# One load for all sample histories in a hybrid convolutional decoder step on eight cores

## The chip, the cores and the metric

The kernel runs on all 8 cores of one Trainium2 chip, one program per core on its own part of the data; the cores do not exchange anything. The time of a run is the device time of the slowest core, in microseconds. Three runs of the kernel before gave a median of 884.12 us (883.93 to 884.82). Each core has TensorE (PE, matmuls), VectorE (DVE), ScalarE (ACT), GpSimd (POOL), SyncE (SP) and 16 DMA engines, which all queues share. DMAs are issued here from SP (the hardware queue, no change of type) and from POOL (the software queue, which can turn f32 into bf16 on the way).

## The reference, cut to what matters

Width is 1024, the depthwise kernel has 31 taps. The change touches only branch B's input for the sample sequences: 128 sequences of 8 new tokens, each with 30 carried rows of history.

```python
a_b, a_c, a_h, a_z, b_v, b_g, b_z, gate_a, gate_b = split(rmsnorm(h) @ w_in)
s  = a_c * a_h;  ya = a_b * dwconv3([buf_a, s]) * silu(a_z);          ya = ya @ w_out_a
v  = b_v * sigmoid(b_g)
ext_b = concatenate([buf_b, v], axis=1)      # history rows in front: zeros for prompts, state_conv_b for samples
c  = dwconv31(ext_b) + b_conv_b
yb = (silu(layernorm(c)) * silu(b_z)) @ w_out_b
h  = h + (sigmoid(gate_a) * ya + sigmoid(gate_b) * yb) @ w_o
h  = h + sigmoid(rmsnorm(h) @ w_pg) * (p @ w_pe);   y = rmsnorm(h)
```

## The kernel before, in words

Each core has 2176 tokens: one prompt of 2048 tokens, in four chunks (`si` 0 to 3) of 512 tokens each, and 16 sample sequences with 128 tokens (`si` 4). Channels are in 8 blocks `j` of 128. The order of all work is the order in which the Python code calls `S.add`; each engine runs its own instructions in that order and waits on semaphores for the others, so an instruction that waits holds everything behind it on its engine.

- **Start (0 to about 73 us).** x tiles are loaded into `xs1`, scaled to bf16 in `xb1`, transposed by PE and stored as `uT`. Both buffers lie in the upper half of `cb`, which is not yet in use. Between the tiles PE does the first projections.
- **v projections.** `s2_proj(j, si)` multiplies chunk `si` by the two weight tiles of block `j` (slots of the ring of 8, loaded by POOL), DVE forms v (L535) in `vrow`, and SP stores it to DRAM (`vd<-t_vrow`). Blocks 0 to 3 are done first (the loop over `PIECES`), blocks 4 to 7 are interleaved with the convolution. When the last chunk of block `j` is projected, `wdone` frees its two ring slots and `pump` issues the next two weight loads on POOL.
- **The convolution** works on `v8[j % 2]`, which has a row for each 16 channels times 8 phases, in 8 groups q, of 340 columns: 4 zeros, 256 of the prompt (`t_v<-vd`, SP, L566), and columns 260 to 339 for the samples, 16 sequences times 5. Of the five, the first four are history and the last is the new token. `hist_load(j)` (L557, POOL) loads all 80 columns from DRAM; then a DVE copy, `conv_samples(j)` (L578, L580), overwrites every fifth with the new token from `vs8`. `conv_half(j, hh)` (L596, L604) does 20 matmuls per half, 16 halves in all; ACT copies the result (L611) and SP moves it into `cb` (`t_cb<-t_c`). `v8` has two buffers, so block `j` can be loaded only when the convolution of block `j - 2` has been read by PE.
- The list `POS` (L1058) sets after which of the 20 projection jobs each half stands. `conv_samples(0)` stands ahead of the third job's projection, `s2_proj(4, 1)`; the first half stands right behind that projection.
- `swq` (L337) lets at most 6 DMAs of the software queue be under way: each waits until the sixth before it has landed.
- **Afterwards** come branch A with its taps, the LayerNorm statistics, the output projections and the last stage by token tiles (about 731 us to the end). None of that code is changed.

`alias(new, old)` makes the first writer of a name wait for all that used the old names of the same memory.

Of the kernel before, what the change touches and what calls it, by code (L numbers as in the profile page):

```python
# [8 lines left out]
BF16 = mybir.dt.bfloat16  # L9
# [4 lines left out]
NCH = 8  # L14
# [3 lines left out]
NTOK = 2176  # L18
# [5 lines left out]
NPH = 8  # L24
NBL = 256
NQ = 8
# [130 lines left out]
def build_program():  # L157
    nc = bass.Bass("TRN2", target_bir_lowering=False)

    def din(name, shape):  # L160
        return nc.dram_tensor(name, shape, F32, kind="ExternalInput").ap()
# [4 lines left out]
    x_d = din("x", [NTOK, D])  # L166
    pT_d = din("pT", [128, 2, NTOK])
    sa_d = din("sa", [128, NCH, 32])
    h8_d = din("h8", [NCH, 128, NQ, 80])
    sbh_d = din("sbh", [352, D])  # L170
    w_in = din("w_in", [72, 128, D])
    w_oa = din("w_oa", [8, 128, D])
# [21 lines left out]
    with contextlib.ExitStack() as st:  # L194
# [5 lines left out]
        def at(name, shape, dt, off):  # L200
            n = size_of[dt]
            for s in shape[1:]:
                n *= s
            assert off % 32 == 0 and off + n <= SIZE - 64, (name, off, n)
            return nc.alloc_sbuf_tensor_at("t_" + name, shape, dt, offset=BASE + off)
# [3 lines left out]
        def take(n):  # L209
            o = cur[0]  # L210
            cur[0] += (n + 31) // 32 * 32
            return o

        def sb(name, shape, dt):
            n = size_of[dt]
            for s in shape[1:]:
                n *= s
            return at(name, shape, dt, take(n))
# [3 lines left out]
        o_cb = take(NCH * NTOK * 4)  # L222
# [35 lines left out]
        v8 = [sb(f"v8{i}", [128, NQ, 340], BF16) for i in range(2)]  # L258
# [25 lines left out]
        o_r4 = o_cb + 4 * NTOK * 4  # L284
        NXS = 6
        xs1 = [at(f"x1{i}", [128, D], F32, o_r4 + 4096 * i) for i in range(NXS)]
        NXB = 4
        xb1 = [at(f"xb1{i}", [128, D], BF16, o_r4 + 4096 * NXS + 2048 * i) for i in range(NXB)]
        X1_RES = [f"x1{i}" for i in range(NXS)] + [f"xb1{h}{i}" for i in range(NXB) for h in ("", "h")]


# [15 lines left out]
        S = Sched(nc)  # L307
# [3 lines left out]
        def balloc():  # L311
            return free_banks.pop(0)
# [24 lines left out]
        def swq():  # L337
            r = f"swq{swq_ctr[0] % SWQ}"
            swq_ctr[0] += 1
            return r  # L340

        def pdma(out, in_, reads, writes, key):
            S.add("pool", lambda e: e.dma_start(out=out, in_=in_), reads=reads, writes=list(writes) + [swq()], dma=key)  # L343

        def sdma(out, in_, reads, writes, key):
            S.add("sp", lambda e: e.dma_start(out=out, in_=in_), reads=reads, writes=writes, dma=key)  # L346
# [49 lines left out]
        def wgroup():  # L396
            g = gnext[0]
            gnext[0] += 1
            assert all(t in slot_of for t in WG[g]), "weight tile not prefetched"
            return g, [slot_of[t] for t in WG[g]]  # L400

        def wdone(g):
            for t in WG[g]:
                ring_free.append(slot_of[t])
            pump()
# [7 lines left out]
        def proj(b, k_ring, si, o=0, n=None):  # L413
            n = n or CHUNKS[si][1]
            tt = range(4 * si + o // 128, 4 * si + (o + n) // 128)
            res = [f"uT{t}" for t in tt], [f"uT{t}" for t in tt] + [f"uTh{t}" for t in tt]
            mm8(b, k_ring, lambda k: uT[si][:, k, o:o + n], lambda k: res[k // 4], n)
# [136 lines left out]
            bfree(bg, bv)  # L554


        def hist_load(j):  # L557
            s = j % 2
            pdma(v8[s][:, :, 260:340], h8_d[j], [], [f"v8{s}h"], f"v8{s}h")

        def conv_load(j):
            s = j % 2
            if j >= 2:
                hist_load(j)
            if j < 7:
                sdma(v8[s][:, :, 4:260], vd[j].rearrange("c (a m) -> (c a) m", m=NBL).rearrange("(q r) m -> r q m", r=128),  # L566
                     [f"vd{j}_{si}" for si in range(4)], [f"v8{s}p"], f"v8{s}p")
            else:
                for q in range(NQ):
                    sdma(v8[s][:, q, 4:260], vrow[16 * q:16 * q + 16, :].rearrange("c (a m) -> c a m", m=NBL),  # L570
                         [f"vst{i}" for i in range(NVST)], [f"v8{s}p"] if q == 0 else [f"v8{s}p{q}"], f"v8{s}p{q}")
# [5 lines left out]

        def conv_samples(j):  # L578
            s = j % 2
            S.add("dve", lambda e: e.tensor_copy(out=v8[s][:, :, 264:340:5], in_=vs8[s][:]),  # L580
                  reads=[f"vs8{s}"], writes=[f"v8{s}h"])
            if j + 2 < NCH:
                vs_pend.append(j + 2)
# [140 lines left out]
        def s3_job(j, si):  # L724
            off, n = CHUNKS[si]
            if j not in s3w:
                s3w[j] = wgroup()
            g, (kh, kc, kz, kb) = s3w[j]
            bh, bc, bz, bb = [balloc() for _ in range(4)]
            for b, kk in ((bh, kh), (bc, kc), (bz, kz), (bb, kb)):  # L730
                proj(b, kk, si)
            if si == 4:
                wdone(g)
            th = talloc()
            S.add("act", lambda e: e.activation(out=tmp[th][:, 0:n], in_=ps[:, bh, 0:n], func=AF.Copy),  # L735
                  reads=[f"ps{bh}"], writes=[f"tmp{th}"])
            if si < 4:
                sdst, sres = sxf[:, 512 + off:512 + off + n], f"sx{si}"
            else:
                S.add("pool", lambda e: e.tensor_copy(out=sexts[:, 0:32], in_=hista[:, j, :]),  # L740
                      reads=["hista"], writes=["sextsh"])
                sdst, sres = sexts[:, 32:160], "sextsn"
            S.add("dve", lambda e: e.tensor_tensor(out=sdst, in0=ps[:, bc, 0:n], in1=tmp[th][:, 0:n], op=ALU.mult),  # L743
                  reads=[f"ps{bc}", f"tmp{th}"], writes=[sres])
            if si == 3:
                S.add("pool", lambda e: e.tensor_copy(out=sx[:, 0:2, 1:NBL], in_=sx[:, 8:10, 0:NBL - 1]),
                      reads=["sx3"], writes=["sxh"])
                S.add("pool", lambda e: e.tensor_copy(out=skeep[:, j, :].unsqueeze(2), in_=sx[:, 8:10, NBL - 1:NBL]),
                      reads=["sx3"], writes=[f"skeep{j}"])
            if si == 4:  # L750
                S.add("pool", lambda e: e.tensor_copy(out=skeep_s[:, j, :], in_=sexts[:, 128:160]),
                      reads=["sextsn"], writes=[f"skeep_s{j}"])
            tz = talloc()
            S.add("act", lambda e: e.activation(out=tmp[tz][:, 0:n], in_=ps[:, bz, 0:n], func=AF.Silu),
                  reads=[f"ps{bz}"], writes=[f"tmp{tz}"])
            if si == 3:
                zap, zres = bzh[:, 0:n], "bzh"
            else:
                zap, zres = tmp[tz][:, 0:n], f"tmp{tz}"
            S.add("dve", lambda e: e.tensor_tensor(out=zap, in0=ps[:, bb, 0:n], in1=tmp[tz][:, 0:n], op=ALU.mult),  # L760
                  reads=[f"ps{bb}", f"tmp{tz}"], writes=[zres])
            bfree(bh, bc, bz, bb)
            if si != 3:
                taps(j, si, zap, zres)
            if si == 2:
                taps(j, 3, bzh[:], "bzh")
# [262 lines left out]
        for p, (si, o, n, prep) in enumerate(PIECES):  # L1029
            for j in range(4):  # L1030
                if si == 3 and 1 <= j < 3:
                    conv_load(j - 1)
                s2_proj(j, si, o, n)
                if si == 3 and o + n == 512:
                    wdone(s2w[j][0])
                if prep[j]:
                    s1_step()
                if si == 3 and o == 0 and builds:
                    w_build(*builds.pop(0))
                if si == 2 and o == 0 and j < 2:  # L1040
                    hist_load(j)
                    vs_load(j)
            if p == 0:
                S.add("pool", lambda e: e.memset(onesf, 1.0), writes=["onesf"])
                S.add("pool", lambda e: e.memset(epsc[:], LN_EPS), writes=["epsc"])
                for i in range(2):
                    S.add("pool", lambda e, i=i: e.memset(v8[i][:, :, 0:4], 0.0), writes=[f"v8{i}z"])
                for j in range(4):
                    vsd_store(j)
                pdma(mask[:], mask_d, [], ["mask"], "mask")  # L1050
                pdma(tw.rearrange("p a b -> p (a b)"), tw_d, [], ["tw"], "tw")
                sdma(hista[:], sa_d, [], ["hista"], "hista")
        S.alias([f"cq{q}_{g}" for q in range(4, 8) for g in range(NQ)] + [f"c{q}_4" for q in range(4, 8)], X1_RES)

        jobs = [(j, si) for j in range(4, 8) for si in (4, 0, 1, 2, 3)]
# [51 lines left out]


        conv_samples(7)
        s3_job(0, 3)  # L1110
        for _ in range(2):
            half()
# [50 lines left out]
        j = NCH - 1  # L1163
# [131 lines left out]
```

How the kernel before makes its waits and increments, by code:

```python
            def run(engname, e):  # L113
                waited = {}
                for o in ops:
                    if o["eng"] != engname:
                        continue
                    need = {}
                    for d in o["deps"]:
                        od = ops[d]
                        v = od["seq"] * (16 if od["dma"] is not None else 1)
                        if v > need.get(od["chan"], 0):
                            need[od["chan"]] = v
                    for c, v in need.items():
                        if waited.get(c, 0) >= v:
                            continue
                        e.wait_ge(sems[c], v)
                        waited[c] = v
                    ins = o["fn"](e)
                    if o["signal"]:
                        ins.then_inc(sems[o["chan"]], 16 if o["dma"] is not None else 1)
                if engname == final_wait_eng:
                    for c, v in final.items():
                        if waited.get(c, 0) < v:
                            e.wait_ge(sems[c], v)
```

## Time and profile before

| | us |
|---|---|
| median of 3 runs | 884.12 |
| the profiled execution's own time | 888.18 |
| span of its slowest core (core 1) | 886.6 |
| span of the other cores | 877.5 to 883.7 |
| PE busy on core 1 | 855.5 (96%) |
| DVE, ACT, POOL busy on core 1 | 508.5, 301.1, 145.0 |

The page and the timelines below are those of core 1 unless a core is named. A span runs from the first to the last instruction of a core; the profiled execution's own time is longer than the span by 1.6 us. PEclk (the granted clock) is 1.00 at 2.4 GHz. "t_v" is `v8`, "t_vs" is `vs8`, "t_ring" the weight ring; buffer numbers are left out in the trace. The DMA share is the mean over 16 engines of the time that packets took; it exceeds 1 where packets of both queues are under way at once.

### The profile page before, as it was taken

To read this page: it belongs to the slowest core of one execution; us is meant where nothing else is said; L and a number is where in the kernel's file an instruction comes from. 1 tells how busy PE (TensorE), PEld (TensorE's weight loads), DVE (VectorE), ACT (ScalarE), POOL (GpSimd) and SP (SyncE) were. 2 spreads that over 40 slices of the span, in tenths; PEclk is the share of its full clock that TensorE was granted. 3 is DMA by queue.
4 is the path that set the end of the run, shared out by engine and by line. 5 is a ranking of instruction groups with operands and counts; after the bars stand their busy time and mean duration, and the time that the engine had idled before them with its cause. 6 is when DMAs were issued, how large, how long until landed. Compare 5 with 4: busy or idle time off the path is not lost.

```text
span 886.6 us, 15264 instructions; the slowest of 8 cores (877.5 to 886.6 us)
## 1 busy us (share of the span) xinstructions
PE 855.5 (96%) x4970; PEld 443.1 (50%) x4970; DVE 508.5 (57%) x791; ACT 301.1 (34%) x565; POOL 145.0 (16%) x274
## 2 busy tenths in 40 slices
PE   7999988999999999999999999999999999999993
PEld 4886544555444545454554444444445444444441
DVE  2455334566997777777777733333333235777775
ACT  4773223355344332423323321111111112444442
POOL 3142101100101101010210101110001001344441
PEclk9999999999999999999999999999999999999997
DMA  9977999987302123030313155521222044867642
GB/s 196 260 145 100 163 154 193 148 134 110 81 0 48 24 37 60 13 61 1 60 17 57 18 161 95 96 39 33 48 48 42 13 96 101 207 172 181 175 126 95
DMA packets 93964, 84.42 MB, mean 95 GB/s; under 512 B 53280, under 2 KB 74784, under 8 KB 93344
## 3 DMA queue, kind: packets, MB, share of 16 engines
q1 hardware_dynamic: 66112, 52.29, 25.2%
q0 software_dynamic: 27776, 31.17, 23.8%
q8 instruction: 41, 0.67, 0.3%
q14 instruction: 35, 0.29, 0.1%
HBM read 86.80 MB, written 15.61 MB: 116 GB/s over the span
## 4 chain that ended last, share of the span: by engine, by line
PE 85%; DMA 5%; SPq 3%; issue 2%; ACT 2%; DVE 2%; POOL 1%; DVEq 0%; POOLq 0%; ACTq 0%
PE ps L409 67%; PE ps L849 7%; PE ps L870 6%; SPq L346 3%; PE ps L604 3%; PE ps L876 1%; DMA t_v<-vd 1%; DMA vd<-t_vrow 1%; DMA t_x<-x 1%; PE ps L672 1%; DMA t_ring<-w_ob 1%; ACT t_xb L484 0%; PE ps L498 0%; DMA t_cb<-t_c 0%; ACT t_xb L424 0%
## 5 line engine op out<-in xcount | busy, mean ns | idle before, releaser
L409 PE MATMUL ps<-t_uT,t_ring 128*128 128x512 bf16 (+2 forms) x3200 | 543.5, 330 | 0.9 <-DMA t_ring<-w_in 0.7
L409 PEld LDWEIGHTS ps<-t_uT,t_ring 128*128 128x128 bf16 x3200 | 279.6, 98 | 252.5 <-issue 3.0
L823 DVE TENSOR_TENSOR t_tmp<-ps,t_tmp 128x512 f32<-128x512 f32 (+1 forms) x80 | 48.7, 610 | 151.7 <-PE ps L409 151.1
L343 POOL DMA_DIRECT2D t_ring<-w_in x72 | 38.8, 540 | 392.4 <-PE ps L409 389.6
L820 ACT ACTIVATE t_tmp<-ps 128x512 f32<-128x512 f32 (+1 forms) x80 | 42.3, 532 | 177.6 <-PE ps L409 177.6
L781 ACT ACTIVATE t_tmp<-t_tmp,t_vid 128x512 f32<-128x512 f32 (+1 forms) x40 | 29.9, 749 | 125.0 <-DVE t_tmp L778 125.0
L535 DVE TENSOR_TENSOR t_vrow<-ps,t_tmp 128x512 bf16<-128x512 f32 (+2 forms) x52 | 25.2, 485 | 79.1 <-PE ps L409 34.1
L409 PE MATMUL ps<-t_cb,t_ring 128*128 128x512 bf16 (+1 forms) x320 | 65.4, 347 | 0.3 <-DMA t_ring<-w_ob 0.3
L409 PE MATMUL ps<-t_yaT,t_ring 128*128 128x512 bf16 (+1 forms) x320 | 65.4, 347 | 0.0
L849 PE MATMUL ps<-t_wo_t,t_cb 128*128 128x512 bf16 x272 | 61.5, 379 | 0.0
L870 PE MATMUL ps<-t_wpg_t,t_u2T 128*128 128x512 bf16 x256 | 57.9, 379 | 0.0
L604 PE MATMUL ps<-t_v,t_Wp 128*128 128x336 bf16 x320 | 49.4, 312 | 7.6 <-DMA t_v<-vd 6.6
L714 DVE SCALAR_TENSOR_TENSOR t_tmp<-t_sx,t_vid,t_tmp 128x512 f32<-128x512 f32 x64 | 48.1, 751 | 6.7
L426 POOL TENSOR_SCALAR t_msq<-t_ssq 128x1 f32<-128x1 f32 x50 | 22.9, 458 | 136.7 <-ACT t_yt L424 54.4
L409 PEld LDWEIGHTS ps<-t_cb,t_ring 128*128 128x128 bf16 x320 | 28.9, 98 | 30.7 <-issue 0.8
L604 PEld LDWEIGHTS ps<-t_v,t_Wp 128*128 128x128 bf16 x320 | 31.4, 99 | 25.7 <-issue 9.7
L409 PEld LDWEIGHTS ps<-t_yaT,t_ring 128*128 128x128 bf16 x320 | 29.0, 98 | 30.2
L743 DVE TENSOR_TENSOR t_sx<-ps,t_tmp 128x512 f32<-128x512 f32 x32 | 22.1, 689 | 37.0 <-ACT t_tmp L735 31.6
L849 PEld LDWEIGHTS ps<-t_wo_t,t_cb 128*128 128x128 bf16 x272 | 26.6, 98 | 31.9
L870 PEld LDWEIGHTS ps<-t_wpg_t,t_u2T 128*128 128x128 bf16 x256 | 25.0, 98 | 30.2
L611 ACT ACTIVATE t_c<-ps 128x512 f32<-128x512 f32 x32 | 19.1, 597 | 57.7 <-PE ps L604 35.3
L528 ACT ACTIVATE t_tmp<-ps 128x128 f32<-128x128 f32 (+2 forms) x60 | 23.5, 406 | 32.1 <-PE ps L409 31.8
(99 smaller groups left out, 755.1 us busy)
## 6 DMA issues: line engine op xcount, KB each, us to landing
t_ring<-w_in POOLq DMA_DIRECT2D x72, 256.0 KB, 5.9
t_x<-x SPq DMA_DIRECT2D x17, 512.0 KB, 8.6
t_xs<-x SPq DMA_DIRECT2D x17, 512.0 KB, 5.7
t_cb<-t_c SPq DMA_DIRECT2D x64, 128.0 KB, 6.5
y<-t_yt SPq DMA_DIRECT2D x16, 512.0 KB, 3.7
vd<-t_vrow SPq DMA_DIRECT2D x28, 128.0 KB, 4.6
t_v<-vd SPq DMA_DIRECT2D x7, 512.0 KB, 10.1
t_ring<-w_oa POOLq DMA_DIRECT2D x8, 256.0 KB, 5.9
```

The costliest lines, as they stand in the source:

```text
L343: S.add("pool", lambda e: e.dma_start(out=out, in_=in_), reads=reads, writes=list(writes) + [swq()], dma=key)
L346: S.add("sp", lambda e: e.dma_start(out=out, in_=in_), reads=reads, writes=writes, dma=key)
L409: S.add("pe", lambda e, k=k: e.matmul(ps[:, b, 0:n], lhsT=ring[k_ring][:, k, :], rhs=rhs_fn(k), start=(k == 0), stop=(k == NCH - 1)), read ...
L528: S.add("act", lambda e: e.activation(out=tmp[tg][:, 0:n], in_=ps[:, bg, 0:n], func=AF.Sigmoid), reads=[f"ps{bg}"], writes=[f"tmp{tg}"])
L535: S.add("dve", lambda e: e.tensor_tensor(out=vst[q][:, o:o + n], in0=ps[:, bv, 0:n], in1=tmp[tg][:, 0:n], op=ALU.mult), reads=[f"ps{bv}", ...
L604: S.add("pe", lambda e, b=b, qq=qq, q=q, d=d: e.matmul(ps[:, b, 0:NWIN], lhsT=Wp[w][:, qq * NLAG + d, :], rhs=v8[s][:, q, 4 - d:4 - d + NWIN],
L714: S.add("dve", lambda e, k=k: e.scalar_tensor_tensor(out=tmp[t2][:, 0:n], in0=tp[k], scalar=vecs[:, V_WCA + 3 * j + k:V_WCA + 3 * j + k + ...
L781: S.add("act", lambda e: e.activation(out=tmp[tx][:, 0:n], in_=tmp[tx][:, 0:n], func=AF.Silu, scale=vcol(V_LNG, j), bias=vcol(V_LNB, j)), ...
L820: S.add("act", lambda e, p=p, t=t: e.activation(out=tmp[t][:, 0:n], in_=ps[:, p, 0:n], func=AF.Sigmoid), reads=[f"ps{p}"], writes=[f"tmp{t}"])
L823: S.add("dve", lambda e, p=p, t=t: e.tensor_tensor(out=tmp[t][:, 0:n], in0=ps[:, p, 0:n], in1=tmp[t][:, 0:n], op=ALU.mult), reads=[f"ps{p} ...
L849: S.add("pe", lambda e, h=h, b=b, k=k: e.matmul(ps[:, b, :], lhsT=cbb[:, k, mcol:mcol + 128], rhs=wo_t[:, k, 512 * h:512 * h + 512], start ...
L870: S.add("pe", lambda e, h=h, b=b, k=k: e.matmul(ps[:, b, :], lhsT=u2T[t % 3][:, k, :], rhs=wpg_t[:, k, 512 * h:512 * h + 512], start=(k == ...
```

## The change

The eight history loads, with 80 columns for each of 8 groups (short runs of 160 bytes in bf16), are replaced by one load of all histories for all blocks. The host packs only the four history columns of each sequence, in the order in which they are kept, so each partition gets one contiguous run of 4096 values (16 KB of f32 in DRAM, 8 KB of bf16 in SBUF). The load goes into `hst`, a new tile over the last 8 KB of `cb`, which lies over three of the `xb1` buffers of the start. It is issued on POOL after the loop over `PIECES`. `conv_samples(j)` gets a second DVE copy ahead of the old one, which moves the 512 history values per partition from `hst[:, j]` into `v8`. The last block's results in `cb` wait for the last reader of `hst`.

```diff
--- before.py
+++ after.py
@@ -166,7 +166,7 @@
     x_d = din("x", [NTOK, D])
     pT_d = din("pT", [128, 2, NTOK])
     sa_d = din("sa", [128, NCH, 32])
-    h8_d = din("h8", [NCH, 128, NQ, 80])
+    h8_d = din("h8", [128, NCH * NQ * 64])
     sbh_d = din("sbh", [352, D])
     w_in = din("w_in", [72, 128, D])
     w_oa = din("w_oa", [8, 128, D])
@@ -286,6 +286,10 @@
         xs1 = [at(f"x1{i}", [128, D], F32, o_r4 + 4096 * i) for i in range(NXS)]
         NXB = 4
         xb1 = [at(f"xb1{i}", [128, D], BF16, o_r4 + 4096 * NXS + 2048 * i) for i in range(NXB)]
+
+        hst = at("hst", [128, NCH, NQ, 16, 4], BF16, o_cb + NCH * NTOK * 4 - NCH * NQ * 128)
+        assert o_cb + NCH * NTOK * 4 - NCH * NQ * 128 >= o_r4 + 4096 * NXS + 2048
+        HST_UNDER = [f"xb1{h}{i}" for i in range(1, NXB) for h in ("", "h")]
         X1_RES = [f"x1{i}" for i in range(NXS)] + [f"xb1{h}{i}" for i in range(NXB) for h in ("", "h")]
 
 
@@ -554,14 +558,12 @@
             bfree(bg, bv)
 
 
-        def hist_load(j):
-            s = j % 2
-            pdma(v8[s][:, :, 260:340], h8_d[j], [], [f"v8{s}h"], f"v8{s}h")
+        def hist_load():
+            S.alias(["hst"], HST_UNDER)
+            pdma(hst.rearrange("p j q s b -> p (j q s b)"), h8_d, [], ["hst"], "hst")
 
         def conv_load(j):
             s = j % 2
-            if j >= 2:
-                hist_load(j)
             if j < 7:
                 sdma(v8[s][:, :, 4:260], vd[j].rearrange("c (a m) -> (c a) m", m=NBL).rearrange("(q r) m -> r q m", r=128),
                      [f"vd{j}_{si}" for si in range(4)], [f"v8{s}p"], f"v8{s}p")
@@ -577,6 +579,9 @@
 
         def conv_samples(j):
             s = j % 2
+            S.add("dve", lambda e: e.tensor_copy(
+                out=v8[s][:, :, 260:340].rearrange("p q (s b) -> p q s b", b=5)[:, :, :, 0:4], in_=hst[:, j]),
+                reads=["hst"], writes=[f"v8{s}h"])
             S.add("dve", lambda e: e.tensor_copy(out=v8[s][:, :, 264:340:5], in_=vs8[s][:]),
                   reads=[f"vs8{s}"], writes=[f"v8{s}h"])
             if j + 2 < NCH:
@@ -1038,7 +1043,6 @@
                 if si == 3 and o == 0 and builds:
                     w_build(*builds.pop(0))
                 if si == 2 and o == 0 and j < 2:
-                    hist_load(j)
                     vs_load(j)
             if p == 0:
                 S.add("pool", lambda e: e.memset(onesf, 1.0), writes=["onesf"])
@@ -1050,6 +1054,7 @@
                 pdma(mask[:], mask_d, [], ["mask"], "mask")
                 pdma(tw.rearrange("p a b -> p (a b)"), tw_d, [], ["tw"], "tw")
                 sdma(hista[:], sa_d, [], ["hista"], "hista")
+        hist_load()
         S.alias([f"cq{q}_{g}" for q in range(4, 8) for g in range(NQ)] + [f"c{q}_4" for q in range(4, 8)], X1_RES)
 
         jobs = [(j, si) for j in range(4, 8) for si in (4, 0, 1, 2, 3)]
@@ -1107,6 +1112,7 @@
 
 
         conv_samples(7)
+        S.alias([f"cq7_{g}" for g in range(NQ)] + ["c7_4"], ["hst"])
         s3_job(0, 3)
         for _ in range(2):
             half()
@@ -1266,8 +1272,8 @@
         m["sa"] = f(sa[s0:s0 + 16].transpose(2, 1, 0).reshape(8, 128, 32).transpose(1, 0, 2))
         hist = np.zeros((16, 40, D), np.float32)
         hist[:, 2:32] = sbuf[s0:s0 + 16]
-        h8 = hist.reshape(16, 5, NPH, NCH, NQ, 16).transpose(3, 5, 2, 4, 0, 1)
-        m["h8"] = f(h8.reshape(NCH, 128, NQ, 80))
+        h8 = hist[:, 0:32].reshape(16, 4, NPH, NCH, NQ, 16).transpose(5, 2, 3, 4, 0, 1)
+        m["h8"] = f(h8.reshape(128, NCH * NQ * 64))
         m["sbh"] = f(sbuf[s0:s0 + 16, 8:30].transpose(1, 0, 2).reshape(352, D))
         in_maps.append(m)
     if "nc" not in _CACHE:
```

POOL, around the load; the names are the tiles, `t_v80` and `t_v81` the two `v8`, `vsd4` the new tokens of block 4 on their way to DRAM. Before:

```order
L343 DMA t_v80_83<-h8 128x8x80 [waits s_d_vsd0]
L426 TENSOR_SCALAR t_msq_56<-t_ssq_55 128x1 [waits s_act]
L429 TENSOR_TENSOR t_rsd_57<-t_msq_56,t_mhalf_52 128x1 [waits s_pool]
L343 DMA t_v81_84<-h8 128x8x80 [waits s_d_vsd1]
L426 TENSOR_SCALAR t_msq_56<-t_ssq_55 128x1 [waits s_act]
L429 TENSOR_TENSOR t_rsd_57<-t_msq_56,t_mhalf_52 128x1 [waits s_pool]
L343 DMA t_ring0_65<-w_in 128x1024 [waits s_pe,s_d_vsd2]
```

and a few rows on, at the end of the eight ring loads:

```order
L343 DMA t_ring7_72<-w_in 128x1024 [waits s_pe,s_d_ring1]
L343 DMA vsd4<-t_vkeep_s_59 128x128 [waits s_d_ring2,s_dve]
L343 DMA t_v80_83<-h8 128x8x80 [waits s_pe,s_d_ring3,s_dve]
L343 DMA t_ring0_65<-w_in 128x1024 [waits s_pe,s_d_ring4]
L343 DMA t_ring1_66<-w_in 128x1024 [waits s_pe,s_d_ring5]
```

The same second place on POOL now:

```order
L347 DMA t_ring6_71<-w_in 128x1024 [waits s_d_ring0,s_pe]
L347 DMA t_ring7_72<-w_in 128x1024 [waits s_d_ring1,s_pe]
L347 DMA t_hst_110<-h8 128x4096 [waits s_d_ring2]
L347 DMA vsd4<-t_vkeep_s_59 128x128 [waits s_d_ring3,s_dve]
L347 DMA t_ring0_65<-w_in 128x1024 [waits s_pe,s_d_ring4]
L347 DMA t_ring1_66<-w_in 128x1024 [waits s_pe,s_d_ring5]
```

The two histories of blocks 0 and 1 stood ahead of the eight ring loads; the one load stands behind them, and behind the PE work that each ring load waits for. The six later history loads, which waited for PE, are gone.

DVE, at the samples of blocks 0 and 1, before:

```order
L535 TENSOR_TENSOR t_vrow_82<-ps,t_tmp1_74 128x512 [waits s_d_vst0,s_pe,s_act,s_dve]
L541 TENSOR_TENSOR t_vkeep_58<-ps,t_tmp1_74 128x8
L580 COPY t_v80_83<-t_vs80_94 128x8x16 [waits s_d_v80h,s_d_vs80]
L535 TENSOR_TENSOR t_vrow_82<-ps,t_tmp2_75 128x512 [waits s_d_vst1,s_pe,s_act,s_dve]
L541 TENSOR_TENSOR t_vkeep_58<-ps,t_tmp2_75 128x8 [waits s_dve]
L580 COPY t_v81_84<-t_vs81_95 128x8x16 [waits s_d_v81h,s_d_vs81]
```

and now:

```order
L539 TENSOR_TENSOR t_vrow_82<-ps,t_tmp1_74 128x512 [waits s_pe,s_dve,s_act,s_d_vst0]
L545 TENSOR_TENSOR t_vkeep_58<-ps,t_tmp1_74 128x8
L582 COPY t_v80_83<-t_hst_110 128x8x16x4 [waits s_d_hst]
L585 COPY t_v80_83<-t_vs80_94 128x8x16 [waits s_dve,s_d_vs80]
L539 TENSOR_TENSOR t_vrow_82<-ps,t_tmp2_75 128x512 [waits s_pe,s_act,s_d_vst1]
L545 TENSOR_TENSOR t_vkeep_58<-ps,t_tmp2_75 128x8
L582 COPY t_v81_84<-t_hst_110 128x8x16x4
L585 COPY t_v81_84<-t_vs81_95 128x8x16 [waits s_dve,s_d_vs81]
```

The first copy for block 0 waits for the whole of the one load (`s_d_hst`), with the v of the next projection behind it; the later ones wait for no load of history.

## Rows read from the trace of the kernel before

**Rows 1.** Spans and granted clock of the cores, in the profiled execution.
```profile
core 0: 877.5 us, clock 0.994
core 1: 886.6 us, clock 0.990
core 2: 883.7 us, clock 0.993
core 5: 881.5 us, clock 0.993
```
**Rows 2.** Windows, core 1: us, busy of PE, PEld, DVE, ACT, POOL; PEclk, DMA share, GB/s.
```profile
110.00:120.00 10.00, 9.28 (x67) 5.59 (x65) 3.96 (x7) 3.51 (x10) 1.78 (x3) 1.00 1.54 169
260.00:500.00 240.00, 240.00 (x1299) 116.43 (x1298) 181.17 (x313) 82.45 (x151) 27.28 (x55) 1.00 0.21 35
```
**Rows 3.** Timeline of PE, core 1: start us, us, engine, line [idle before].
```profile
96.43 3.02 PE L604 MATMUL ps<-t_v,t_Wp 128*128 128x336 bf16 x20
...
123.05 3.02 PE L604 MATMUL ps<-t_v,t_Wp 128*128 128x336 bf16 x20 [3.77 <-DMA t_v<-vd]
...
152.31 4.43 PE L604 MATMUL ps<-t_v,t_Wp 128*128 128x336 bf16 x20 [2.84 <-DMA t_v<-vd]
...
175.29 3.02 PE L604 MATMUL ps<-t_v,t_Wp 128*128 128x336 bf16 x20 [0.98 <-DVE t_vkeep_s L549]
```
**Rows 4.** Timeline of PE, core 2: the same columns.
```profile
97.11 3.02 PE L604 MATMUL ps<-t_v,t_Wp 128*128 128x336 bf16 x20 [0.56 <-DMA t_v<-vd]
122.30 4.69 PE L604 MATMUL ps<-t_v,t_Wp 128*128 128x336 bf16 x20 [2.34 <-DMA t_v<-vd]
```
**Rows 5.** Timeline of PE, core 5.
```profile
121.21 3.02 PE L604 MATMUL ps<-t_v,t_Wp 128*128 128x336 bf16 x20 [1.77 <-DMA t_v<-vd]
```
**Rows 6.** Timeline of POOL, core 1.
```profile
89.34 0.53 POOL L343 DMA_DIRECT2D t_ring<-w_in  x1 [1.20 <-PE ps L409]
...
106.44 0.89 POOL L343 DMA_DIRECT2D t_v<-h  x1 [15.21 <-PE ps L604]
...
132.99 0.88 POOL L343 DMA_DIRECT2D t_v<-h  x1 [13.38 <-PE ps L604]
```
**Rows 7.** Issues of window 530:600, core 1: line engine op xcount, KB each, us to landing.
```profile
t_wo_t<-w_o POOLq DMA_DIRECT2D x2, 1024.0 KB, 11.3
```
**Rows 8.** Last line of the answers on t_wpg_t of core 1 and t_wo_t of core 2.
```profile
DMA to landing us min/median/max: 8.3/10.9/13.4
DMA to landing us min/median/max: 14.7/14.8/15.0
```
**Rows 9.** Timeline of DVE, core 1.
```profile
94.07 0.34 DVE L580 COPY t_v<-t_vs 128x128 bf16<-128x128 bf16 x1
...
117.09 0.35 DVE L580 COPY t_v<-t_vs 128x128 bf16<-128x128 bf16 x1 [5.54 <-DMA t_v<-h]
...
130.07 0.35 DVE L580 COPY t_v<-t_vs 128x128 bf16<-128x128 bf16 x1 [8.46 <-DMA t_v<-h]
...
174.81 0.33 DVE L580 COPY t_v<-t_vs 128x128 bf16<-128x128 bf16 x1
```
**Rows 10.** Groups of DVE by form, 0 to 260 us: xcount, busy us, mean ns, idle.
```profile
L503 DVE TENSOR_TENSOR t_uT<-ps,t_vid 128x512 bf16<-128x512 bf16 x6 | 3.8, 681 | 3.3 <-PE ps L498 3.3
```
**Rows 11.** DMA queue of window 122:135, core 1: packets, MB, share of 16 engines.
```profile
q0 software_dynamic: 970, 0.16, 19.5%
```
**Rows 12.** The same of window 530:600, core 1.
```profile
q0 software_dynamic: 2044, 5.36, 41.6%
```
**Rows 13.** Issues of window 104:112, core 1: KB each, us to landing.
```profile
t_v<-vd SPq DMA_DIRECT2D x1, 512.0 KB, 13.9
t_v<-h POOLq DMA_DIRECT2D x1, 160.0 KB, 10.5
```
**Rows 14.** Windows, core 1, at the time of the new load (columns as in rows 2).
```profile
94.00:96.00 2.00, 2.00 (x11) 0.88 (x9) 0.41 (x3) 0.60 (x1) 0.00 (x0) 1.00 1.03 160
96.00:98.00 2.00, 2.00 (x14) 1.24 (x13) 0.00 (x0) 0.00 (x0) 0.00 (x0) 1.00 0.53 88
```

## The prediction

> **What bounds the kernel now.** I read the spans of the cores first, then the windows, then PE's timeline and the timelines of whatever PE waited for. Core 1 is the slowest at 886.6 us, the other slow ones are at 881.5 to 883.7, and the fastest is at 877.5 [rows 1]. All run the same program, so the nine microseconds between them are waits and not work. In the windows PE is busy all the time from 260 to 500 us with the DMAs at a fifth [rows 2]: there nothing but PE counts, and no edit of this change lies there. The stretch that matters is 90 to 210 us, where projections and convolution halves alternate. From 110 to 120 us the DMA share is 1.54 and PE loses 0.7 of 10 us [rows 2], so there the DMAs bound the end of some waits. PE's timeline shows which: on core 1 it stands 3.77 us before the half at 123.05 and 2.84 us before that at 152.31, both times for the prompt's columns of `v8`, and every core has a wait of 0.98 us like that at 175.29, for DVE [rows 3]. Core 2 has 2.34 us, core 5 1.77 [rows 4, 5]. A wait also costs clock in some cases: 20 matmuls of a half take 3.02 us, but 4.43 after the wait at 152.31 and 4.69 after core 2's; after the longer one at 123.05 still 3.02 [rows 3, 4]. The first half of all, at 96.43, has no idle time before it [rows 3]: its histories are issued ahead of the ring loads.
>
> **What the change removes.** Eight history loads. In the window from 122 to 135 us the software queue carries hardly anything but history (one is issued at 132.99 [rows 6], the one before it ends early in the window): 970 packets, 0.16 MB, 19.5% of 16 engines over 13 us [rows 11]. That is 0.195 x 13 x 16 = 40.6 engine-us, or 42 ns for a packet of 160 bytes; a load of 1024 such packets takes 43 engine-us, 2.7 us of all 16 engines. Eight loads: 21.5 us of all 16. Four of them are issued between 106.44 and 146 us (the first and the third in [rows 6]), in the stretch where PE waits for `t_v<-vd`. The one behind core 1's first wait needs 13.9 us to land, and a history load under way beside it 10.5 [rows 13]. Take that load away and the prompt's columns come 2.7 us earlier (its engine time once) to 5.4 (that twice, the next load running beside it too); PE's wait was 3.77. I count nine tenths of core 1's waits and of the clock lost by the second as gone: 0.9 x (3.77 + 2.84 + 1.41) = 7.2 us. On core 2 it is the 2.34 us and 4.69 - 3.02 = 1.67 us of clock, 4.0 in all, on core 5 1.8. The bounds are nothing and all of it.
>
> By the Trainium skill ("DMA: Bandwidth & Descriptors", Specifications) a DMA write wants at least 512 bytes, since below that the engine reads, modifies and writes; this speaks for the change, and the small packets here move 160 B in 42 ns, 3.8 GB/s per engine, where those of the window from 530 to 600 us move 5.36 MB in 466 engine-us, 11.5 GB/s [rows 11, 12].
>
> DVE also waits 5.54 and 8.46 us for histories at 117.09 and 130.07 [rows 9]. These waits go as well, but PE stood for `t_v<-vd` and not for them, so they are worth nothing beyond the above. On POOL 8 issues become one, and its waits for PE at the history loads go; its ring loads wait for PE anyhow.
>
> **What it adds: the load itself, at a late place.** The new load has 1.05 MB in bf16. From the window of large software loads, 0.416 x 70 x 16 = 466 engine-us for 5.36 MB [rows 12] is 87 engine-us per MB, so the load takes 91 engine-us, 5.7 us of all 16 engines. It stands on POOL behind the eight ring loads. The last of these is issued at 89.34 and takes 0.53 [rows 6], so the new one goes out at 89.9. The limit of six makes it wait for the third ring load, which went out five steps of 0.53 + 1.20 us [rows 6] before the last and has landed. It is needed before the half at 96.43.
>
> How long it takes to land is the main unknown. The same shape, 128 rows of 8 KB, is loaded four times later: two loads of w_o land in 11.3 us on core 1 and 14.7 to 15.0 on core 2, two of w_pg in 8.3 and 13.4 [rows 7, 8]. The 8.3 is a load with nothing ahead of it. At 89.9 there is a queue: three ring loads and block 0's prompt columns are still under way, and the share is 1.03 until 96 us [rows 14]. Only from 96 it falls to 0.53 [rows 14], and at 98 the columns of block 1 follow. So the w_o rows, which have ring loads ahead of them too, are nearer. I take 12.5 us, with 8.3 and 15.0 as the ends. It lands at 102.4.
>
> Behind the landing stand on DVE the new copy, then the old one (0.34), then a gap of 0.15 us to PE (174.81 + 0.33 to 175.29) [rows 3, 9]. The new copy moves 512 bf16 values per partition, with every fifth place skipped. The trace has no such copy. The old one, of 128 values, takes 0.34 [rows 9], and a 512-value bf16 operation on DVE 0.68 [rows 10]; these are the bounds, and I take 0.7, since its length is that of the second. PE goes on at 102.4 + 0.7 + 0.34 + 0.15 = 103.6 in place of 96.4: **7.2 us of a new wait, on every core** (3.1 and 9.7 at the ends). Nothing covers it: PE's next instruction is the half, and DVE's queue behind the copy holds the v of the job before, so its store comes later by as much.
>
> The clock: of three waits of 2.3 to 3.8 us, two were followed by 1.4 and 1.7 us of slow matmuls and one by none [rows 3, 4]. After twice that wait I take 1.5 us, with 0 and 3.1 (both rows together) as the ends.
>
> The other seven copies cost DVE 7 x 0.7 = 5 us, of which one counts: at 174.81 PE already waits 0.98 us for DVE, which ends the old copy at 175.14 [rows 3, 9]. The new copy stands straight ahead of the old one, so **0.7 us more on every core**. Block 7's `cb` rows wait for the last copy, which comes before block 7's convolution: nothing.
>
> **Sum**, in the spans of the profiled execution. Every core gets 7.2 + 1.5 + 0.7 = 9.4. Core 1: 886.6 + 9.4 - 7.2 = 888.8. Core 2: 883.7 + 9.4 - 4.0 - 0.56 (its wait at 97.11 is within the new one) = 888.5. Core 5: 881.5 + 9.4 - 1.8 = 889.1. The cores come together at about 889, and with the 1.6 us around the span a profiled execution would show 890.7. The profiled execution of before took 888.18, 4.06 above the median of 884.12. Most of this I put down to core 1's waits, since without core 1 the slowest span is core 2's 883.7, which with 1.6 is 885.3, only 1.2 above the median. These waits are gone in the new sum, so I take off 1.2 and not 4.06: **889.5 us, 0.6% slower**. (Took one off 4.06, it would be 886.6.)
>
> **The rivals.** I call a difference under 0.2%, 1.8 us, no change: about what a measurement of this kernel can tell.
>
> *A short landing.* The load lands in 8.3 us, as the first of w_pg did, and the clock isn't lost. Then every core gets 3.1 + 0.7 = 3.8; core 1 comes to 883.2, core 2 to 882.9, core 5 to 883.5, about the 883.7 of core 2 before: 884, no change. For it: the DMAs run dry at 96 to 98 us [rows 14]. Against it: the ring loads ahead, and core 2's 15 us for the same shape. The Trainium skill ("DMA: Bandwidth & Descriptors", Anatomy of one DMA — SWDGE path) gives 2.0 us plus bytes over 436 GB/s; for the 2.1 MB that are read this is an estimate of 6.8 us, and the sum would be 1.5 us lower still. The trace contradicts it for this shape, with 8.3 at best.
>
> *The relief wins, faster.* With one mechanism, the waits for `t_v<-vd`: if in the timed runs the slowest core is one like core 1, which loses 3.77 + 2.84 + 1.41 = 8.0 us to them, and they all go, then with a landing of 8.3 us the net is 3.8 - 8.0 = -4.2: 880. It decides from the point where new wait, clock and 0.7 are together under 8.0, a landing of 12.6 us with no clock lost. Against it: the three runs agree within 0.9 us, so random long waits on one core don't set them, and in the profile core 2 has 4.0 us to win and core 5 1.8.
>
> *Worse contention.* The load lands in 15 us or more on the slow cores, the ring loads and block 0's prompt columns are held up by it, and the clock costs 3.1: 9.7 + 3.1 + 0.7 = 13.5 on core 5, less 1.8, is a span of 893.2 and a run of 893.6.
>
> **How the numbers follow.** The forecast, a landing of 10 to 14.5 us and its spread of clock and relief, gives 886.5 to 892.5: 0.62. Worse contention, 892 to 896: 0.15. Short landing, 882.5 to 887: 0.15, of which 0.03 is slower, 0.11 the same and 0.01 faster. The relief wins, 879 to 882: 0.08. Together slower 0.80, same 0.11, faster 0.09. The range, 884 to 894.5, leaves out the winning relief, half of the short landings that are below and the far end of contention, about 0.2.
>
> **What the changed kernel's profile would show.** PE idle 5 to 10 us before its first half at 96, put down to the load of `hst` or the copy; the first of the new copies waiting for that DMA, 0.7 us long, the others waiting for no DMA; after that half perhaps 4.4 to 4.7 us for 20 matmuls. `t_v<-vd` near 115 us lands in under 11 us and no wait of PE behind it is above 1. DVE's wait at the half near 183 is 1.7 us in place of 0.98. The software queue has some 8000 packets fewer. I am wrong if PE's wait at the first half is under 4 us (a landing under 9), if waits for `t_v<-vd` stay as they were (then the time is up to 4 us above), or if another wait takes their place.

## The result: 897.45 us in place of 884.47, 1.4% slower

The changed kernel takes 897.45 us (median of 4 runs, 896.52 to 898.26) and the kernel before, on the same chip, 884.47 (4 runs, 883.93 to 885.60). The ratio is 1.0139, with a 95% interval of 1.0126 to 1.0153. The forecast was 889.5, with a range of 884 to 894.5: the direction was right, the size was not, and the time lies 3 us outside the range. Runs in which the cores of one die were granted a clearly lower clock are left out of every median and ratio here.

**The profile after.** The profiled execution took 897.86 us. All cores now lie close together, where before they ran from 877.5 to 886.6 [rows 1]. The answer on the cores of the changed kernel:

```profile
core 0: 894.2 us, clock 0.985
core 1: 891.8 us, clock 0.989
core 2: 892.8 us, clock 0.989
...
core 5: 895.2 us, clock 0.985
...
core 7: 891.7 us, clock 0.987
```

So every core got something new that is alike on all of them. PE's timeline of core 5, the slowest, is the counterpart of [rows 3] and [rows 5] (start us, us, engine, line, operation, in brackets the idle time before it and what ended it):

```profile
69.26 0.61 PE L502 MATMUL ps<-t_idb,t_xb 128*128 128x128 bf16 x8 [0.31 <-ACT t_xb L488]
...
73.65 23.52 PE L413 MATMUL ps<-t_uT,t_ring 128*128 128x256 bf16 x128
...
109.14 5.35 PE L609 MATMUL ps<-t_v,t_Wp 128*128 128x336 bf16 x20 [11.96 <-DVE t_vrow L539]
...
182.30 3.02 PE L609 MATMUL ps<-t_v,t_Wp 128*128 128x336 bf16 x20 [1.44 <-DVE t_vkeep_s L553]
```

There is one wait of 11.96 us before the first half, that half takes 5.35 us in place of 3.02, and then comes the known wait for DVE, 1.44 in place of 0.98. Nothing else: the waits of up to 3.77 us for `t_v<-vd` at later halves [rows 3 to 5] are gone on all cores. On the eight cores the first wait is 10.6 to 12.3 us and the half behind it 4.32 to 5.75.

The releaser that PE's row names is a `t_vrow` on DVE, which has itself been held up. DVE's timeline of core 5 shows by what:

```profile
107.65 0.35 DVE L582 COPY t_v<-t_hst 128x512 bf16<-128x512 bf16 x1 [12.85 <-DMA t_hst<-h]
108.17 0.35 DVE L585 COPY t_v<-t_vs 128x128 bf16<-128x128 bf16 x1 [0.17 <-DVE t_v L582]
108.41 0.69 DVE L539 TENSOR_TENSOR t_vrow<-ps,t_tmp 128x512 bf16<-128x512 f32 x1
```

The new copy waits 12.85 us for the one load, the old copy and the v of the last projection stand in the queue behind it. The chain of waits of core 5 (start us, us, what) passes through the same four pieces:

```profile
90.43 17.12 DMA t_hst<-h
107.65 0.36 DVE t_v L582
108.41 0.70 DVE t_vrow L539
109.14 5.35 PE ps L609 x20
```

The load, issued at 90.43 as forecast, takes **17.12 us** to land and not 12.5. Over the cores it is 15.9 to 17.5. The windows of core 5 show why (us, busy of PE, PEld, DVE, ACT, POOL, then PEclk, DMA share, GB/s). First the kernel before:

```profile
80.00:90.00 10.00, 10.00 (x60) 5.04 (x59) 6.09 (x9) 2.07 (x4) 3.15 (x6) 1.00 0.96 147
90.00:98.00 8.00, 8.00 (x42) 3.92 (x41) 2.31 (x7) 1.19 (x2) 0.56 (x2) 1.00 0.88 166
98.00:106.00 8.00, 8.00 (x50) 4.62 (x48) 2.17 (x4) 2.65 (x7) 0.00 (x0) 1.00 0.96 199
```

and the changed kernel:

```profile
90.00:98.00 8.00, 7.17 (x37) 3.14 (x34) 1.44 (x5) 1.48 (x3) 1.50 (x3) 1.00 1.07 184
98.00:106.00 8.00, 0.00 (x0) 0.00 (x0) 0.00 (x0) 0.00 (x0) 0.00 (x0) 0.64 1.01 199
...
106.00:108.00 2.00, 0.00 (x0) 0.00 (x0) 0.35 (x1) 0.00 (x0) 0.00 (x0) 0.50 0.47 117
```

Before, the 16 DMA engines already worked 0.88 x 8 + 0.96 x 8 = 14.7 of the 16 us from 90 to 106. The load wants 5.7 us of them (the prediction's estimate), and they did 1.07 x 8 + 1.01 x 8 = 16.6: only 1.9 us more. There was little room for it, and PE stood until it was through. A share of 1 is no hard ceiling, since it was 1.54 from 110 to 120 us on core 1 [rows 2]; but the bytes say the same. By the GB/s of these rows 2.9 MB moved in the 16 us before and 3.1 MB now, 0.1 MB more for a load of 1.05 MB. The second thing in these rows is the clock: PE stood idle from 97.18 on, and the granted clock is 0.64 on average from 98 to 106 and 0.50 from 106 to 108, the lower of its two levels (1.2 GHz).

The load also delays what stands ahead of it. The last ring load, issued half a microsecond earlier, landed in 9.1 to 9.7 us on the eight cores before, and lands in 10.6 to 12.8 us now. Issues of core 5 (KB each, us to landing); `t_v<-vd` here is block 1's:

```profile
t_hst<-h POOLq DMA_DIRECT2D x1, 1024.0 KB, 17.1
t_v<-vd SPq DMA_DIRECT2D x1, 512.0 KB, 8.9
...
t_ring<-w_in POOLq DMA_DIRECT2D x1, 256.0 KB, 12.1
```

And block 0's columns, issued 4 to 5 us before it on SP's queue, take 18.3 us on core 3 and 19.6 on core 7 (8.5 to 13.5 on the eight cores before). Core 7:

```profile
t_v<-vd SPq DMA_DIRECT2D x1, 512.0 KB, 19.6
```

So a later load isn't served behind the earlier ones, but in part beside them. On these two cores the columns are there only at 103 and 104 us, 1.5 to 2 us before the history. By these times PE, free at 96, would have stood there for some 7 us even if nobody had needed the new load.

### The profile page after: what moved, and what is told of

Same layout as the page of the kernel before. It is cut to its first block, busy times and chain, and to the rows that moved or that the text cites. A ratio compares the mean times of both kernels' runs of the same rounds, so it can differ in the third digit from the quotient of the medians.

```text
span 895.2 us, 15236 instructions; the slowest of 8 cores (891.7 to 895.2 us)
## 1 busy us (share of the span) xinstructions
PE 857.5 (96%) x4970; PEld 443.5 (50%) x4970; DVE 511.5 (57%) x799; ACT 302.2 (34%) x565; POOL 136.5 (15%) x267
## 2 busy tenths in 40 slices
DMA packets 85788, 84.15 MB, mean 94 GB/s; under 512 B 44976, under 2 KB 66480, under 8 KB 85040
## 4 chain that ended last, share of the span: by engine, by line
PE 86%; DMA 6%; DVE 2%; issue 2%; ACT 2%; POOL 1%; DVEq 0%; SPq 0%; POOLq 0%; ACTq 0%
PE ps L413 66%; PE ps L854 7%; PE ps L875 6%; PE ps L609 5%; DMA t_x<-x 2%; DMA t_hst<-h 2%; PE ps L881 1%; DMA vd<-t_vrow 1%; PE ps L677 1%; DMA t_ring<-w_in 1%; ACT t_xb L428 0%; DMA t_cb<-t_c 0%; PE ps L502 0%; ACT t_xb L488 0%; DVE t_tmp L719 0%
```

## The experiments

Ratios are against the kernel before on the same chip, 884.5 to 885.0 us. "Early" means POOL's queue at 70 us, ahead of the eight ring loads; "late" is where the change has the load. Theory A: the price is the late place alone, and the relief is real. Theory B: the megabyte is a burden wherever it goes.

**1. The load early** (`e_early`). One line moved:

```diff
+                if p == 3 and j == 1:
+                    hist_load()
...
-        hist_load()
```

> The one load is issued on POOL at about 70 us, ahead of the eight ring loads; all else as in the changed kernel. Theory A (the 13 us come from PE waiting for a load that lands 17 us after its issue behind a DMA backlog, 11 to 12 us, with 1.3 to 2.7 us of slow clock behind it): the load lands by 82, no wait at the first half, 881 to 883.5 us, since the relief for the later waits stays and 0.5 us of the new DVE copy stays. Theory B (the amount of the load or the copies cost the time wherever they stand): above 890 us.

887.42 us (11 runs), ratio 1.0030 (1.0012 to 1.0048): 10 us of the 13 are won back, but both expectations missed. The load lands in 9.9 to 12.8 us, long before it is needed, and nobody waits for it. But PE now waits 2.8 to 3.8 us at the first half, on every core, for block 0's columns. Core 0's PE, and the landing of these columns (issues of window 84:90):

```profile
99.59 5.76 PE L609 MATMUL ps<-t_v,t_Wp 128*128 128x336 bf16 x20 [3.39 <-DMA t_v<-vd]
```

```profile
t_v<-vd SPq DMA_DIRECT2D x1, 512.0 KB, 13.3
```

Its windows say that the DMA engines don't get a pause between 70 and 98 us:

```profile
70.00:80.00 10.00, 9.95 (x71) 6.50 (x71) 5.71 (x13) 2.76 (x6) 1.89 (x4) 1.00 0.88 131
80.00:90.00 10.00, 9.95 (x59) 5.02 (x59) 5.68 (x10) 1.98 (x4) 3.17 (x6) 1.00 1.04 173
90.00:98.00 8.00, 6.14 (x28) 2.64 (x27) 1.37 (x4) 1.20 (x2) 0.54 (x1) 1.00 0.93 175
```

So the load was moved, and the next transfer that PE needs became late.

**2. No history at all** (`e_none`). The load is left out and `hst` is zeroed by POOL at 71 us, so the histories are missing from the result; the DVE copies stay.

```diff
-            pdma(hst.rearrange("p j q s b -> p (j q s b)"), h8_d, [], ["hst"], "hst")
+            S.add("pool", lambda e: e.memset(hst[:], 0.0), writes=["hst"])
```

> Leaves the histories out: the tile is set to zero by POOL at about 70 us in place of being loaded, the eight DVE copies stay. What is left against the kernel before is the relief of eight loads and the copies. Theory A: 881 to 883 us, no more than 1 us under the kernel with the early load. If the copies cost more than their 0.5 us at one place, it is above 884.

885.33 us (11 runs), ratio 1.0005 (0.9989 to 1.0022). Theory A missed again: taking away all history traffic wins nothing that can be measured. The later waits are mostly gone, also on cores 3 and 5, where PE doesn't stop at the first half; two cores keep 0.95 and 1.18 us near 122. But block 0's columns still land in 10.2 to 13.3 us, and PE now waits 0.5 to 2.2 us for them at the first half on six cores, where before it waited on two; and all cores have the 0.46 us more of the copies. So leaving out the histories relieves the later halves but not the time: what makes block 0's columns late is something else.

**3. Blocks 0 and 1 by the old loads, the one load late for blocks 2 to 7** (`e_two_old`). Nobody needs `hst` before block 2.

```diff
-            S.add("dve", lambda e: e.tensor_copy(
+            if j >= 2:
+                S.add("dve", lambda e: e.tensor_copy(
...
+                    pdma(v8[j][:, :, 260:340], h8o_d[j], [], [f"v8{j}h"], f"v8{j}h")
```

> The histories of blocks 0 and 1 come again by the two old loads at their old place, without the new copy; the one load stays at its late place and is first needed at block 2's copy, near 112 us. Theory A: the load lands near 107 as before and nobody waits for it, 882 to 885 us. Theory B (a late megabyte delays the transfers that PE needs by itself): PE waits for t_v<-vd grow to 4 us or more, above 888.

891.42 us (3 runs), ratio 1.0074 (1.0045 to 1.0103): theory B's side. Without anybody waiting for it, the late megabyte costs half of what it cost with the wait. Seven cores wait 2.4 to 5.0 us near 122 for `t_v<-vd`. Core 6, the slowest, waits at the first half for block 0's columns, which take 18.7 us there, as on cores 3 and 7 of the changed kernel. Cores 0 and 6:

```profile
125.24 4.69 PE L611 MATMUL ps<-t_v,t_Wp 128*128 128x336 bf16 x20 [4.97 <-DMA t_v<-vd]
```

```profile
104.39 5.47 PE L611 MATMUL ps<-t_v,t_Wp 128*128 128x336 bf16 x20 [7.81 <-DMA t_v<-vd]
```

**4. The load in two, block 0's 128 KB first** (`e_split`), late.

```diff
+            pdma(hst[:, 0:1].rearrange("p j q s b -> p (j q s b)"), h8_d[:, 0:512], [], ["hst"], "hst")
+            pdma(hst[:, 1:8].rearrange("p j q s b -> p (j q s b)"), h8_d[:, 512:4096], [], ["hst7"], "hst7")
```

> At the late place, the histories of block 0 (128 KB in bf16) in a load of their own ahead of the other seven. Theory A with the backlog as the cause (the queue is served in order, some 7 us of engine work ahead, and the load's own 5.7 us behind it): the first lands 11 to 13 us after its issue, the wait falls from 11.5 to about 6.5 us, 891 to 893 us. If a software load at this place has a long time to land whatever its size: still 15 us or more and 896 to 898.

893.48 us (2 runs), ratio 1.0099 (1.0062 to 1.0135), 0.5 us above what the theory of a queue said; its landing of 11 to 13 us came. The first eighth is 0.7 us of engine work (an eighth of the estimate for the whole) and lands in 11.4 to 12.9 us; the first wait is 6.7 to 9.0 us. The issues of core 5:

```profile
t_hst<-h POOLq DMA_DIRECT2D x1, 896.0 KB, 16.6
t_ring<-w_in POOLq DMA_DIRECT2D x1, 256.0 KB, 11.9
t_hst<-h POOLq DMA_DIRECT2D x1, 128.0 KB, 12.3
```

So 12 us of landing come with the place, where the other 896 KB are issued straight behind. But the wait isn't the eighth's on all cores. On five it is put down to DVE's queue behind the copy; on cores 0, 4 and 6, with core 0 the slowest, it is put down to block 0's columns, which take 18.1 to 20.3 us there. Core 4:

```profile
105.48 4.81 PE L610 MATMUL ps<-t_v,t_Wp 128*128 128x336 bf16 x20 [9.00 <-DMA t_v<-vd]
```

Splitting the load doesn't touch that second part of the price.

**5. PE kept busy in the wait** (`e_warm`), by 44 matmuls on old data before the first half, whose result nobody reads.

```diff
+            if j == 0 and hh == 0:
+                bw = balloc()
+                for _ in range(44):
+                    S.add("pe", lambda e: e.matmul(ps[:, bw, :], lhsT=uT[0][:, 0, 0:128], rhs=uT[0][:, 1, :], start=True, stop=True),
```

> The changed kernel with 44 matmuls of 512 columns (9.5 us, results unused) on PE ahead of the first half, while it waits for the one load. If the slow matmuls behind the wait are a price of the idle time, they go: the first 20 matmuls take 3.0 us in place of 4.3 to 5.8, and the time falls by 1.3 to 2.7 us, to 895 us. If the clock has nothing to do with it, 897.5 us or more.

895.21 us (3 runs), ratio 1.0114 (1.0090 to 1.0138): 2.2 us less than the changed kernel, as expected. Cores 0 and 5 stand for the two kinds:

```profile
96.61 9.66 PE L606 MATMUL ps<-t_uT 128*128 128x512 bf16 x43
107.83 3.02 PE L615 MATMUL ps<-t_v,t_Wp 128*128 128x336 bf16 x20 [1.56 <-DVE t_v L585]
```

```profile
108.66 4.63 PE L615 MATMUL ps<-t_v,t_Wp 128*128 128x336 bf16 x20 [2.73 <-DVE t_v L585]
```

Five cores, idle for 1.5 to 2.2 us behind the filler, run the half in 3.02; the three that idle for 2.1 to 2.9 still take 4.5 to 4.6. The five have spans of 890.7 to 892.1, the three 893.1 to 894.1, and one of the three sets the time. So that the slow matmuls are a price of the idle time is shown by the five; what the time of the kernel would gain on all eight is not measured, only that each half with the slow clock costs 1.3 to 2.7 us.

**6. The kernel before, its ring loads spread out** (`b_defer`). Only two of the eight ring loads go out at 77 to 90 us; the others follow in twos behind the stores of blocks 4, 5 and 6, the rest behind block 7's. Histories as before.

```diff
-                    wdone(s2w[j][0])
+                    wdone(s2w[j][0], 2 if j == 0 else 0)
...
-                wdone(s2w[j][0])
+                wdone(s2w[j][0], 8 if j == 7 else 0)
+            if si == 4:
+                pump(4 if j == 7 else 2)
```

> The kernel before, with its eight histories as they were, but only two of the eight ring loads between 77 and 90 us; the other six go out two at a time behind the new tokens of blocks 4, 5 and 6 and the rest behind those of block 7. Theory C (block 0's prompt columns share the DMA engines with eight ring loads and land just when PE needs them, so that any further transfer in 70 to 97 us is paid by PE): they land in 6 to 8 us in place of 8.5 to 13.5, no wait at the first half on any core, the waits near 120 us stay; 882.5 to 884 us. Rival (the ring loads only move their contention to later waits): 884.5 us or more.

885.95 us (11 runs), ratio 1.0014 (1.0000 to 1.0028). The cause was right: block 0's columns, 8.5 to 13.5 us before, now land in 4.1 to 4.5, and no core waits at the first half. The gain was not: waits come up elsewhere, where history loads meet the ring loads that were moved. Core 2:

```profile
133.84 3.02 PE L604 MATMUL ps<-t_v,t_Wp 128*128 128x336 bf16 x20 [2.12 <-DMA t_v<-vd]
...
188.09 8.78 PE L604 MATMUL ps<-t_v,t_Wp 128*128 128x336 bf16 x40 [2.96 <-DMA t_v<-vd]
```

**7. Both: ring loads spread out and the load early** (`e_defer`), the edits of 1 and 6 together.

> The one load early (70 us) and the six ring loads spread as well. Theory C: the 2.8 to 3.8 us before the first half that the early load alone shows on every core are gone, and there are no waits near 120 us; against the early load alone 3.5 to 5 us less, 882 to 884 us. If the early load's wait has another cause than the shared engines (its own landing, the copy), it stays, and the time is 887 us.

882.63 us (12 runs), ratio 0.9974 (0.9961 to 0.9986), as expected: **faster than both kernels**. The whole change, with the room made for it first. Against experiment 6, which differs only in the histories, it is 3.3 us less: once the first half doesn't wait, one load in place of eight does relieve the later halves. The cores lie at 878.2 to 880.0, `t_v<-vd` of block 0 lands in 4.1 to 4.3 us, and but for 0.32 us on core 7 the only wait of PE left between 70 and 260 us is that for DVE. The windows and PE's row of core 5:

```profile
70.00:80.00 10.00, 10.00 (x76) 6.86 (x74) 5.37 (x13) 2.85 (x6) 2.40 (x5) 1.00 0.80 131
80.00:90.00 10.00, 10.00 (x60) 5.01 (x58) 6.12 (x9) 2.07 (x4) 0.00 (x0) 1.00 0.68 159
90.00:98.00 8.00, 8.00 (x42) 3.92 (x40) 2.57 (x8) 1.19 (x2) 1.59 (x3) 1.00 0.82 177
```

```profile
167.56 3.02 PE L609 MATMUL ps<-t_v,t_Wp 128*128 128x336 bf16 x20 [1.41 <-DVE t_vkeep_s L553]
```

**8. The same, block 5's two copies one job earlier** (`e_best`), to take that wait away.

```diff
-                if POS[2 * c] - (c > 0) == i:
+                if POS[2 * c] - (c > 0) - (c == 5) == i:
```

> As the former, and the two copies for block 5 stand one job earlier on DVE, ahead of the sums that hold them up. The wait of 1.44 us near 175 us that all cores have goes: 1.0 to 1.4 us less than the former, about 881.5 us. If another instruction holds PE there, no change.

882.37 us (12 runs), ratio 0.9964 (0.9949 to 0.9978). The wait of 1.4 us is gone on all cores, but some get 0.3 to 1.5 at a half near 195 (core 0):

```profile
195.79 5.87 PE L609 MATMUL ps<-t_v,t_Wp 128*128 128x336 bf16 x40 [1.53 <-DVE t_v L585]
```

Against experiment 7 the 0.3 us can't be told from nothing; the 1.0 to 1.4 us that were expected aren't there. It is the fastest version here, 15 us below the change as it was made.

**9. The load late, but with the ring loads out of its way** (`e_late_clear`): the edits of 6, with the load at its late place.

```diff
-            S.alias(["hst"], HST_UNDER)
+            S.alias(["hst"], HST_UNDER + ["ring7"])
```

> The one load at its late place again (made to wait for the last projection of block 3, so it is issued at about 90 us as in the changed kernel), but with only two of the eight ring loads ahead of it; the other six are spread as in the kernels before. If the backlog of the DMA engines made the load land 16 to 17.5 us after its issue, it now lands in 8 to 10 (the first of w_pg took 8.3), PE waits 3 to 4 us ahead of the first half, and the time is 885.5 to 888 us. If a load of this size at this time is slow by itself, it lands after 13 us or more, and the time is above 891 us.

893.28 us (5 runs, 889.51 to 894.98), ratio 1.0081 (1.0057 to 1.0106). The time is on the side of the second expectation, the landing on most cores nearer to the first, so neither holds as a whole. On seven cores the load lands in 9.8 to 12.7 us and not 15.9 to 17.5, so the ring loads ahead of it are 3 to 7 us of its landing; their spans are 883.8 to 888.3. But core 2 has 16.3 us and a span of 893.4, and it sets the time. The issues of window 86:98, core 7 and core 2:

```profile
t_hst<-h POOLq DMA_DIRECT2D x1, 1024.0 KB, 9.9
t_v<-vd SPq DMA_DIRECT2D x1, 512.0 KB, 15.0
```

```profile
t_hst<-h POOLq DMA_DIRECT2D x1, 1024.0 KB, 16.3
t_v<-vd SPq DMA_DIRECT2D x1, 512.0 KB, 8.6
```

Block 1's columns go out on SP within a microsecond of it, and the two compete: which of them lands first differs from core to core. On six cores the columns take 14.9 to 16.0 us, on core 2 8.6, and on core 3 4.1 with 12.7 for the load. In the other four runs the slowest core (5, 1, 5 and 5) lies at 887.8 to 892.5, so no single core is to blame. What decides the order is open.

## Why the prediction was wrong

The step that failed is the landing of the load: "I take 12.5 us, with 8.3 and 15.0 as the ends". It took 15.9 to 17.5, outside both ends. On core 5 the forecast of the span was 889.1, and it came to 895.2. The 6.1 us between them, term by term:

- *The new wait*: 7.2 forecast, 11.96 measured, 4.8 more. Of this the landing is 4.6. The copy was smaller than taken (0.35 and a gap of 0.17, for 0.7), but PE started 0.6 us behind the old copy and not 0.15. The v that frees PSUM for PE stands in DVE's queue behind the copies; the profile names it on six cores, and the copy on the other two, where the gap is 0.45 all the same. I hadn't counted it.
- *The clock*: 1.5 forecast, 5.35 - 3.02 = 2.33 measured (1.3 to 2.7 over the cores), 0.8 more. Experiment 5 shows its cause.
- *DVE's chain before the later half*: 0.7 forecast, 1.44 - 0.99 = 0.45 measured, 0.25 less.
- *Start and rest*: PE begins 0.4 us later at 69 us already (69.26 against 68.85), and 0.3 us come late in the program; I didn't follow these.
- *The relief*: 1.8 forecast on core 5, 1.77 measured. On core 1 the 7.2 came too. Its mechanism, the histories' small packets, has a part in these waits: they mostly go when the histories are left out (experiment 2), and with the ring loads spread out, eight history loads leave waits of up to 2.96 us (experiment 6) where the one load leaves 0.32 (experiment 7). What the forecast had wrong is that taking them out wins time by itself: in experiment 2 waits for block 0's columns came in their place. In the changed kernel PE's long stop, in which every transfer can catch up, may have helped too; this is argued, not shown.

From the span to the median I added 0.4 (1.6 less 1.2). It is 897.45 - 895.2 = 2.25; with these 1.85 us the whole miss of 7.95 is accounted for. Taking 1.2 off for core 1's waits was not justified: those waits aren't special to the profiled execution. The three runs within 0.9 us, on which the prediction leaned, were too few: 54 runs took 882.3 to 889.6 us. Over these 54 runs of the kernel before, the slowest core lies at 882.8 (median), the fastest at 877.4, and the slowest is another core from run to run.

**Why the landing was misread.** The estimate came from rows of the same shape later in the program, at 8.3 to 15.0 us [rows 7, 8], and from a window with a share of 0.53 [rows 14] that was taken for a gap. The view that decides was at hand and not used: the share over the whole time in which the load must land. From 90 to 106 us it was 0.92 on core 5, room for 1.3 us where 5.7 were wanted, if 1 is taken as full. Two parts of the cause are shown apart. The load shares the engines with what is ahead of it (experiment 9: without the ring loads 3 to 7 us less on seven cores) and with what comes after (the last ring load, 1.3 to 3.2 us later for a load issued behind it; block 1's columns in experiment 9). (One end of the prediction's sum is off in itself: a landing of 8.3 us gives a wait of 3.0 us and not 3.1; nothing hangs on it.) The rival "worse contention", held at 0.15, names this mechanism and gave 893.6; it too took 15 us for the landing, and its band ended at 896. The Trainium skill says ("DMA: Bandwidth & Descriptors", Issuing engines are not separate DMA queues) that DMAs of all issuing engines run on the same 16 DMA engines and interleave. The traces agree: loads of POOL's and SP's queues delay each other in experiments 1, 3 and 9. The Trainium skill's fit for one DMA ("DMA: Bandwidth & Descriptors", Anatomy of one DMA — SWDGE (gpsimd) path), 6.8 us for this load as an estimate, holds in no run here: 9.6 us was the shortest landing of it, in experiment 7.

The sum also had no term for block 0's columns; only the rival had them held up. The late load makes them late in turn. In experiment 3 they hold PE for 7.8 us on core 6, in experiment 4 for 6.7 to 9.0 on three cores, and on cores 3 and 7 of the changed kernel they land nearly as late as the load. So there are two prices of the late place, the wait for the load and the wait for what it delays; experiment 3, without the first, still costs 6.9 us.

**What is left open**: why more cores wait at the first half in experiment 2 than in the kernel before, though less is to be moved; on which cores the late load holds up block 0's columns; and what decides which of two loads issued together lands first.

The signs that the prediction named came in part. The wait at the first half (forecast 5 to 10 us) is 10.6 to 12.3, the slow half and the 8176 packets fewer (93964 to 85788) are there, no copy but the first waits for a DMA, and the new copies take 0.35 us and not 0.7. This is the summary of L582 on core 5 (ns min/median/max, first and last start):

```profile
L582 DVE COPY t_v<-t_hst x8: 341/348/353, 107.6 to 209.9; 128x512 bf16<-128x512 bf16 x8
```

## What to carry to other kernels

Before adding a load, add up the share of the DMA engines over the window in which it must land, in the trace of before. Here the share was near 1, and at both places that were tried the load made something late that PE needed next. First move the transfers that nobody needs yet (here the weights of the next ring), then merge the small ones; either alone won nothing, both together 0.26%. And a DVE copy that waits for a DMA stops everything queued behind it, also what PE waits for.

## What the runs showed of the hardware

- In a stretch with a DMA share near 1, a load of 128 KB, 0.7 us of engine work by estimate, with 896 KB issued behind it, lands in 11.4 to 12.9 us, only some 4 us sooner than one of 1 MB (15.9 to 17.5).
- A load of 1 MB issued 0.5 us later goes with a landing of the one ahead of it on the same queue in 10.6 to 12.8 us in place of 9.1 to 9.7.
- A bf16 copy of 512 values per partition, in runs of four into five places, takes 0.348 us, no longer than one of 128 values with a step of five (0.34 to 0.35); between the two copies into one tile lie 0.17 us.
- After PE's wait of 10.6 to 12.3 us its clock was at the lower level, and 20 matmuls took 4.3 to 5.8 us for 3.02. After 3.8 us of waiting (core 1 in experiment 1) they took 3.02, after 3.4 us (core 0) 5.76: the length of one wait doesn't tell the loss.
